# Output projection of a hybrid encoder layer: sixteen full blocks of w_out, or Strassen's seven half-size products

## The reference

```python
y_r = hr * jax.nn.silu(gr)                       # (tokens, 1024), RG-LRU group
y_c = (v @ cv_w2 + cv_b2) * jax.nn.silu(gc)      # (tokens, 1024), Conformer group
y = concat([y_r, y_c], -1) @ w_out               # w_out is (2048, 1024)
return x + rms_norm(y, post_g)                   # the norm runs over the 1024 outputs of a token
```

## Time and profile before

| | us |
|---|---|
| median of 3 executions | 828.98 |
| lowest and highest | 828.12, 829.11 |
| the profiled execution: its time | 828.99 |
| the profiled execution: its span | 827.0 |
| PE busy in that span | 804.9 |
| DVE, ACT, POOL busy | 571.2, 371.6, 259.0 |

### The profile page before, as it was taken

The page is one execution under the profiler, slowest core; times in us unless marked ns, Lnnn a source line. Parts: engine busy times, 40 slices in busy tenths (PEclk is TensorE's granted clock), DMA queues, the critical chain, the costliest instruction groups (busy, mean ns, idle before and its releaser), DMA issues. The chain is left out here.

```text
span 827.0 us, 12188 instructions
## 1 busy us (share of the span) xinstructions
PE 804.9 (97%) x4964; PEld 783.6 (95%) x4964; DVE 571.2 (69%) x510; ACT 371.6 (45%) x568; POOL 259.0 (31%) x156
## 2 busy tenths in 40 slices
PE   6999999999999999999999989899999999999996
PEld 4999999999999999999999978899999999999996
DVE  6589999999989959959959987962519322212225
ACT  6622482482482482482482458932517212211221
POOL 5224445446456455555464613010110000000000
PEclk8999999999999999999999999999999999999999
DMA  8311212202202302302302300423191111011047
GB/s 276 80 52 52 70 33 78 78 26 77 85 17 77 99 4 77 102 0 77 103 0 77 103 25 1 157 80 100 55 326 52 52 52 52 29 47 51 25 143 276
DMA packets 78737, 65.44 MB, mean 79 GB/s; under 512 B 2587, under 2 KB 71835, under 8 KB 78706
## 3 DMA queue, kind: packets, MB, share of 16 engines
q1 hardware_dynamic: 77776, 63.91, 23.9%
q0 software_dynamic: 928, 1.12, 0.6%
q10 hardware_dynamic: 2, 0.00, 0.0%
HBM read 51.77 MB, written 13.25 MB: 79 GB/s over the span
## 5 line engine op out<-in xcount | busy, mean ns | idle before, releaser
L731 PE MATMUL ps<-act_hi,w_hi 128*128 128x352 f32 (+5 forms) x1320 | 433.8, 329 | 1.1 <-DVE act_lo L1558 0.6
L733 PE MATMUL ps<-act_hi,w_lo 128*128 128x352 f32 (+5 forms) x1320 | 427.8, 324 | 0.0
L732 PE MATMUL ps<-act_lo,w_hi 128*128 128x352 f32 (+2 forms) x1128 | 366.0, 324 | 0.0
L1618 DVE SCALAR_TENSOR_TENSOR ps<-cv_in,par_cv,ps 128x1086 f32<-128x1086 f32 x232 | 313.8, 1353 | 7.8
L731 PEld LDWEIGHTS ps<-act_hi,w_hi 128*128 128x128 f32 x1320 | 248.5, 188 | 7.9 <-issue 6.8
L733 PEld LDWEIGHTS ps<-act_hi,w_lo 128*128 128x128 f32 x1320 | 248.6, 188 | 0.1
L732 PEld LDWEIGHTS ps<-act_lo,w_hi 128*128 128x128 f32 x1128 | 212.6, 188 | 0.4 <-issue 0.3
L586 POOL TENSOR_TENSOR w_lo<-wstage,w_hi 128x1024 fp32r<-128x1024 f32 x40 | 98.5, 2478 | 84.4 <-ACT w_hi L1064 84.2
L1064 ACT ACTIVATE w_hi<-wstage 128x1024 fp32r<-128x1024 f32 x63 | 65.7, 1054 | 101.4 <-PE ps L733 89.6
L1538 DVE TENSOR_TENSOR w_lo<-wstage,w_hi 128x1024 fp32r<-128x1024 f32 x24 | 30.3, 1262 | 60.5 <-ACT w_hi L1064 60.5
L731 PE MATMUL ps<-act_lo,w_hi 128*128 128x416 f32 (+2 forms) x192 | 63.4, 330 | 0.0
(11 more groups left out here) (193 smaller groups left out, 803.9 us busy)
## 6 DMA issues: line engine op xcount, KB each, us to landing
wstage<-in_w_in SPq DMA_DIRECT2D x40, 512.0 KB, 3.8
wstage<-in_w_out SPq DMA_DIRECT2D x16, 512.0 KB, 3.7
silu_spill<-silu_gc SPq DMA_DIRECT2D x8, 528.0 KB, 2.7
yr_spill<-y_rg SPq DMA_DIRECT2D x8, 528.0 KB, 2.7
silu_l<-silu_spill SPq DMA_DIRECT2D x8, 528.0 KB, 3.9
yr<-yr_spill SPq DMA_DIRECT2D x1, 4224.0 KB, 13.1
wstage<-in_cv_w_pw SPq DMA_DIRECT2D x8, 512.0 KB, 4.6
x_in<-in_x_prompt SPq DMA_DIRECT2D x7, 512.0 KB, 6.2
```

The lines of the kernel that those rows point to most:

```text
L731: pe.matmul(out, wh, xh, start=start, stop=False)
L732: pe.matmul(out, wh, xl, start=False, stop=False)
L733: return pe.matmul(out, wl, xh, start=False, stop=stop)
L1618: STT(out=acc, in0=src, scalar=w, in1=acc, op0=ALU.mult, op1=ALU.add).then_inc(taps, 1)
```

## The change

The 2 x 2 blocks (halves of the inputs by halves of the outputs) and the two halves of the tokens (`TH` = 528) are combined by Strassen's scheme: seven products of 1024 x 512 weights with 528 tokens in place of eight. Each product is four steps (`HT` = 4, one per output block), 28 steps in all, each of 8 k x 3 matmuls x 2 chunks of 264 columns. Five products use a sum or difference of two blocks of w_out, formed on POOL in place in one of five stages (`weight_sum`, 20 operations of 128 x 1024). Five use a sum or difference of operand halves, also on POOL (`operand_sum`, 40 operations of 128 x 528). The operand of every product is split anew on ACT and DVE, two k in each step (`next_operand_high`, `next_operand_low`), into `act_hi` and `act_lo` in turn. The first product uses y_r. The results are combined in `c_out` in SBUF: ACT copies, DVE adds or subtracts from PSUM (`add_product`). From step 12 on each step completes half a row: ACT squares it into the PSUM banks of the step, scales it in place, PE turns it (five transposes, `turn_half`), ACT copies the turned half back over the same row. Steps 26 and 27 run as four pieces of 272 and 256 columns.

```diff
-YCH = [(640, 416), (256, 384), (0, 256)]
+PRODUCTS = [((0, 0), ALU.add, (0, 1)), ((0, 1), ALU.subtract, (1, 1)), ((1, 1), None, None),
+            ((0, 0), ALU.add, (1, 1)), ((1, 0), ALU.add, (1, 1)), ((0, 0), None, None),
+            ((1, 0), ALU.subtract, (0, 0))]
+FINAL = 3 * HT
+PAIRED = STEPS - 2
...
+    def b_of(p, k):
+        if p == 1:
+            return c_half(HT + k // 2, k % 2)
+        return [y_r(k, 1), None, y_r(k, 0), y_r(k, 0), y_cv(k, 0), y_r(k, 1), y_cv(k, 1)][p]
...
@@ sync
+            def load_out(i):
+                s, second, (m, h) = BLOCKS[i]
+                if i < N_STAGE:
+                    if i < 2:
+                        sp.wait_ge(late_los, LATE_PW + 7 + i)
+                    elif i < 4:
+                        sp.wait_ge(pw, 6)
+                    else:
+                        sp.wait_ge(st_out, 16 * 6)
+                else:
+                    u, was_second, _ = BLOCKS[i - N_STAGE]
+                    if was_second:
+                        sp.wait_ge(wo_added, weight_sums(u))
+                    else:
+                        sp.wait_ge(late_los, LATE_OUT + u + 1)
...
@@ gpsimd
+            def weight_sum(s):
+                i, op = FIRST_BLOCK[s], PRODUCTS[s // HT][1]
+                if op is not None:
+                    for b in (i, i + 1):
+                        pool.wait_ge(wo_loaded[b % N_STAGE], 16 * (b // N_STAGE + 1))
+                    TT(OUT_STAGE[i % N_STAGE], OUT_STAGE[i % N_STAGE], OUT_STAGE[(i + 1) % N_STAGE], op)\
+                        .then_inc(wo_added, 1)
+            def operand_sum(p, k):
+                if p == 1:
+                    if k == 0:
+                        pool.wait_ge(yr_in, 16)
+                        pool.wait_ge(pw, KT)
+                        pool.wait_ge(yc, KT)
+                    TT(b_of(1, k), y_r(k, 0), y_r(k, 1), ALU.add).then_inc(b_sum, 1)
...
+            weight_sum(0)
+            weight_sum(1)
             pool.wait_ge(st_rows, 2)
...
+            for s in range(STEPS):
+                if s >= 2:
+                    weight_sum(s)
+                for k in (2 * (s % HT), 2 * (s % HT) + 1):
+                    operand_sum(s // HT + 1, k)
...
@@ tensor
+            def bank_free(s):
+                u = s - 2
...
+                elif u // HT in (0, 2):
+                    pe.wait_ge(c_copied, copies(u))
+                elif u // HT == 1:
+                    pe.wait_ge(c_added, additions(u))
+                else:
+                    pe.wait_ge(o_ssq, u - FINAL + 1)
+            for s in range(PAIRED):
+                p, ei = divmod(s, HT)
+                pe.wait_ge(late_los, LATE_OUT + s + 1)
+                bank_free(s)
+                for k in range(KT):
+                    if ei == 0:
+                        pe.wait_ge(b_low, p * KT + k + 1)
+                    for j in range(2):
+                        mm = step_product(s, k, j * TC, TC, 2 * (s % 2) + j)
...
+                    if k == 5 and s > FINAL:
+                        turn_half(s - 1)
@@ scalar
+            out_high(0)
             for k in range(KT):
+                operand_high(0, k)
+            out_high(1)
...
+            for s in range(PAIRED):
+                p, ei = divmod(s, HT)
+                out_high(s + 2)
+                act.wait_ge(oproj, s + 1)
...
+                next_operand_high(s)
@@ vector
+            out_low(0)
+            for k in range(KT):
+                operand_low(0, k)
             pw_out(KT - 1)
+            out_low(1)
+            next_operand_low(-1)
+            for s in range(PAIRED):
+                got = ps[:, 2 * (s % 2):2 * (s % 2) + 2, 0:TC]
+                dve.wait_ge(oproj, s + 1)
+                add_product(s, got)
+                out_low(s + 2)
+                if s >= FINAL:
+                    add_squares(s, got)
+                next_operand_low(s)
...
+                if s > 5 * HT:
+                    y_out(0, s - 5 * HT - 1)
...
+            STT(out=o_last, in0=ps[:, 3, 0:CHUNK_B[1]], scalar=par[:, KT - 1, P_PG:P_PG + 1], in1=c_scaled,
+                op0=ALU.mult, op1=ALU.add).then_inc(last_set, 1)
+            add_chunk(KT - 1, *CHUNK_B, 3, 4)
+            y_out(1, 1)
+            y_out(1, 2)
```

More of the change, by code:

```diff
@@ new lines, in b_hi, with b_lo @@
+    def b_hi(p, k):
+        return (act_hi, act_lo)[p % 2][:, k, 0:TH]
+    def b_lo(p, k):
+        return (act_hi, act_lo)[p % 2][:, k, TH:2 * TH]
+    ssq = [y_r(0, 0), y_r(1, 0)]
+    o_small = [yr[0:16, 2:4, 0:512], yr[0:16, 4:6, 0:512]]
+    X_HOME = [yr[:, 2 * i:2 * i + 2, TH:TH + 512] for i in range(4)] + [yr[0:16, 6:8, 0:512]]
+    for _r in (8, 9, 12, 10, 11):
+        X_HOME.append(act_x[:, _r, 0:D].rearrange("p (a n) -> p a n", a=2))
+    X_HOME[7] = act_x[0:16, 12, 0:D].rearrange("p (a n) -> p a n", a=2)
@@ L551, in _ @@
[L551 to L554, removed]
+            def load_out(i):
[13 more added lines that the diff above has]
+                        sp.wait_ge(late_los, LATE_OUT + u + 1)
+                e = m * HT + s % HT
+                sp.dma_start(OUT_STAGE[i % N_STAGE], w_out_v[:, (1 - h) * KT:(2 - h) * KT, e * P:(e + 1) * P])\
+                    .then_inc(wo_loaded[i % N_STAGE], 16)
@@ L555, in _ @@
+            for i in range(len(BLOCKS)):
+                if BLOCKS[i][0] == 5 * HT + 1 and BLOCKS[i][1] == 0:
+                    sp.wait_ge(b_low, 6 * KT)
+                    load_residual(0)
+                load_out(i)
+            sp.wait_ge(oproj, 6 * HT)
+            load_residual(1)
+            load_residual(2)
+            stores = 0
+            for j, tiles in enumerate(OUT_TILES):
+                for i, (c0, rows) in enumerate(tiles):
+                    n = TILE_BASE[j] + i
                     if j < 2:
@@ L957, in _ @@
                 mm.then_inc(pw, 1)
[L960 to L976, removed]
-                mm.then_inc(o_turned, 1)
@@ L979, in earlier_sums @@
[L979 to L1011, removed]
@@ new lines, in turn_tiles, with sums @@
+            def turn_tiles(j, src, bank):
+                for i, (c0, rows) in enumerate(OUT_TILES[j]):
+                    mm = pe.transpose(ps[0:rows, bank, i * P:(i + 1) * P], src[:, i * P:i * P + rows], ident[:, :])
+                mm.then_inc(o_turned, 1)
+            def sums(j, src, fst, last):
+                for i, (c0, rows) in enumerate(OUT_TILES[j]):
+                    mm = pe.matmul(ps[0:rows, 7, i:i + 1], src[:, i * P:i * P + rows], mean_w[:, 0:1],
+                                   start=fst and i == 0, stop=last, skip_group_check=True)
+                if last:
+                    mm.then_inc(ss_done, 1)
@@ new lines, in last_chunk, with turn_6a @@
+            def last_chunk(s, c0, n, bank, between):
+                for k in range(KT):
+                    mm = step_product(s, k, c0, n, bank)
+                    if k in between:
+                        between[k]()
+                mm.then_inc(oproj, 1)
+            half = STEPS - FINAL - 2
+            c_a = [c_half(e, 1)[:, CHUNK_A[0]:TH] for e in (KT - 2, KT - 1)]
+            c_b = c_half(KT - 2, 1)[:, 0:CHUNK_B[1]]
+            def turn_6a():
+                pe.wait_ge(o_scaled, half + 1)
+                pe.wait_ge(o_placed, half)
+                turn_tiles(1, c_a[0], 4)
@@ new lines, in sums_6a, with sums_turn_7a, turn_6b @@
+            def sums_6a():
+                pe.wait_ge(o_ssq, half + 1)
+                pe.wait_ge(ss_root, 5)
+                sums(1, ssq[1][:, CHUNK_A[0]:TH], True, False)
+            def sums_turn_7a():
+                pe.wait_ge(last_sqd, 1)
+                sums(1, last_sq[1], False, True)
+                pe.wait_ge(o_scaled, half + 2)
+                turn_tiles(1, c_a[1], 6)
+            def turn_6b():
+                pe.wait_ge(o_scaled, half + 3)
+                pe.wait_ge(o_placed, half + 1)
+                turn_tiles(2, c_b, 4)
@@ new lines, in sums_6b @@
+            def sums_6b():
+                pe.wait_ge(o_ssq, half + 2)
+                pe.wait_ge(ss_root, 5 + 3)
+                sums(2, ssq[1][:, 0:CHUNK_B[1]], True, False)
+            pe.wait_ge(late_los, LATE_OUT + PAIRED + 1)
+            pe.wait_ge(o_ssq, PAIRED - 2 - FINAL + 1)
+            last_chunk(PAIRED, *CHUNK_A, 0, {5: lambda: turn_half(PAIRED - 1)})
+            pe.wait_ge(late_los, LATE_OUT + PAIRED + 2)
+            pe.wait_ge(o_ssq, PAIRED - 1 - FINAL + 1)
+            last_chunk(PAIRED + 1, *CHUNK_A, 2, {5: turn_6a})
@@ L1512, in roots, with place_a @@
+            def place_a(e, bank):
+                A(c_half(e, 1)[:, 2 * P:4 * P], ps[:, bank, 0:2 * P], ACT.Copy)
+                A(o_small[1][:, e // 4, e % 4 * P:(e % 4 + 1) * P], ps[0:16, bank, 2 * P:3 * P], ACT.Copy)\
+                    .then_inc(o_placed, 1)
             def roots(j):
                 act.wait_ge(ss_done, j + 1)
-                n, whole = tile_base[j], sum(rows == P for c0, rows in out_tiles[j])
+                n, whole = TILE_BASE[j], sum(rows == P for c0, rows in OUT_TILES[j])
```

(63 more changed lines are left out.)

457 lines of the change are left out of this document (247 added, 210 removed).

## The result

The changed kernel took 839.38 us (median; 838.71 to 840.58) against 829.05 of the kernel before: a ratio of 1.0128 (95% interval 1.0112 to 1.0144), 1.3% slower. The forecast was 823.5 with a range of 814 to 835. The span of the profiled execution is 837.0 us, 10.0 more than before.

A forecast was written before the change was run, and what follows sets the result against it. PE's stream of matmuls was taken to set the end of the projection. Terms -22.7 + 3.5 + 1.6 + 4.0 + 3.7 + 1.6 + 1.0 + 1.8 = -5.5 us on 827.0 gave 823.5, range 814 to 835.

The forecast's parts named there:

- Middle: Later steps, including 16 to 19, 21 and 22: ACT, DVE and load delays mostly hidden, +1.0 us, bounds 0 and 6.
- PE's own work: PE's matmuls, transposes and small sums in the projection: 174.7 us after the change, -22.7 us.
- The start: Steps 0 to 7: later first weights, waits ahead of steps 1 and 2, slower steps 3 to 7, one clock loss.
- The wait of 1.6 ahead of step 1: Ahead of step 1: DVE's low weight part, behind other splits and against an operand sum, comes late, +1.6 us.
- The wait ahead of step 2: Ahead of step 2: late state transfers delay loads and POOL's operand sums delay its weight sum, +4.0 us.
- The turns: Steps 3 to 7: POOL and DVE alternate operation by operation, 6.6 us a step in place of 5.83, +3.7 us.
- The clock: Wait ahead of step 0 or 2: PE's granted clock falls to half pace once, +1.6 us.
- The tail: After the last matmul: DVE's scaled columns, add, y_out, copy and reciprocals delay the final outputs, +1.8 us.
- DVE as the bound: Rival: DVE's queue, waiting for whole POOL operations, sets 7.7 us in steps 3 to 7 and 16 to 19; 835, chance 0.22.
- The hidden turns: Rival: POOL runs at its faster pace, 5.8 us a step, no loss in steps 3 to 7; 815, chance 0.18.
- Short waits: Clock rival: waits ahead of steps 1 to 7 each bring a 1.6 us slow stretch; three more make 828.3, chance 0.07.
- Matmuls of 264 columns: Forecast 121 ns each; rival: they cost 138 ns and eat the gain, about 846, chance 0.03.

The follow-up runs named there:

- Experiment 1: Changed kernel with SP issuing the residual loads of the first output tiles 5 weight blocks later, ahead of step 25's block: 826.69 us, ratio 0.9972.
- experiment 3: Changed kernel with the edits of experiment 1 and experiment 2 together: 821.84 us, ratio 0.9917.
- experiment 2: Changed kernel with the first two w_out blocks loaded ahead of the yr reload and state transfers issued ahead of POOL's second weight sum: 833.19 us.
- experiment 5: On top of experiment 3, POOL forms the weight sum of step 2 ahead of the first four operand sums: 820.10 us, ratio 0.9889.
- experiment 6: On top of experiment 3, operand sums of products 2, 3, 5 and 6 over 16 of 528 columns, leaving out computation: 818.69 us.
- experiment 7: On top of experiment 3, DVE's low operand parts for products 1 and 2 over 16 of 528 columns, leaving out computation: 818.83 us.
- Experiment 4: Changed kernel with 40 idle transposes on PE ahead of step 0 and 24 ahead of step 2: 839.41 us, ratio 1.0118.

## Why the prediction was wrong

**The step that failed** stands under Middle: "Loads have a round of 3.7 + 2.4 + 1.1 + 1.2 = 8.4 us in two steps, 11.7: hidden", and with it the +1.0 with bounds 0 and 6. I priced the round of a load but not the queue that issues it. On SP the residual of the first tiles, with its own wait for the split of product 5, stands ahead of the weights of step 21, and I never listed that move. Measured: step 20 takes 17.9 us in place of 6.4. From step 8 to the last pieces it is 812.65 - 685.50 = 127.2 us, where 5 steps of 5.88 and 13 of 6.42 make 112.9. That is 14.3 over; 1.1 of it are the small sums of step 21, which belong to PE's own work, so 13.2 stand in place of the forecast's 1.0 (0.7 of them in step 18). Experiment 1 moved that wait and won 12.9 us. The prediction had named a wait of PE for scaled rows in steps 12 to 25 as a sign that it was wrong, and that is the wait that came, but from a cause that it had not thought of.

**PE's own work** was right: -22.7 forecast. By the measured paces 13 x 5.88 + 13 x 6.42 + 1.1 + 15.5 (the last pieces, 812.65 to 828.12) = 176.5 against 197.4: -20.9. Of the 1.8 us between them about 1.2 lie in the 26 steps, which took 159.9 in place of 158.7 with their transposes.

**The start** was forecast at 3.5 + 1.6 + 4.0 + 3.7 + 1.6 = 14.4 us and took 685.50 - 622.32 - 8 x 5.88 = 16.1. The 16.1 are 6.3 ahead of step 0, 2.3 in step 0, 3.2 in step 1 with the wait behind it, 1.6 in step 2 and 2.7 in steps 3 to 7. The size held, but not each cause, and that the errors nearly cancel is luck. PE came to step 0 some 0.8 us later than in the kernel before, and the wait ahead of it was 5.5 in place of 3.5: POOL's second weight sum did go ahead of DVE, the case for which the prediction had 627 and which it did not take, and DVE's subtraction beside it took 3.16 us in place of 1.23.

```profile
624.69 3.16 DVE L2009 TENSOR_TENSOR w_lo<-wstage,w_hi 128x1024 fp32r<-128x1024 f32 x1 [7.20 <-ACT w_hi L1613]
```

```profile
624.42 2.35 POOL L832 TENSOR_TENSOR w_stage<-w_stage 128x1024 f32<-128x1024 f32 x1 [0.90 <-DMA w_stage<-in_w_out]
...
634.21 6.93 POOL L842 TENSOR_TENSOR c_out<-yr 128x528 f32<-128x528 f32 x4 [4.41 <-DVE conv_out L1982]
641.11 2.37 POOL L832 TENSOR_TENSOR stage<-stage,wstage 128x1024 f32<-128x1024 f32 x1
```

The wait of 1.6 ahead of step 1 did not come, since step 0 ran slowly; in experiment 3, where step 0 has the full clock, it is there with 1.50. The wait ahead of step 2 was 3.1 in place of 4.0, and not for the states to land: POOL went from its four operand sums straight into `weight_sum(2)` at 641.11. Experiments 2, 3 and 5 say the same: issuing the states earlier left the wait, and moving the sum moved step 2 by 1.74 us but step 8 only by 0.42. From POOL's first operand sum on, the turns of POOL and DVE set step 8.

**The turns** were right: 6.6 us a step forecast, 6.63 to 6.66 measured in steps 4 to 6; experiments 5, 6 and 7 show them. As a term they cost 2.7 us in steps 3 to 7 (32.1 - 5 x 5.88) where 3.7 were forecast, since steps 3 and 7 took only 6.19 and 5.96. The rule of the Trainium skill (SBUF — State Buffer, SBUF: two separate sides), by which whichever of the two starts first blocks the other for the whole instruction, gives 7.7 by the prediction's prices; the rows of steps 5 and 6 say 6.6, and there the measurement decides. That the two hold each other up, as the page says, experiments 6 and 7 confirm.

**The clock** was mis-sized by its number, not its mechanism: one slow stretch of 1.6 us forecast, three seen, one behind each long wait. Step 2 took 1.6 us longer than 5.88, the size forecast, and step 0 took 2.3 longer. The Trainium skill's warning (TensorE: Matmul & The Clock Gate, HAM oscillation — how this bites in real kernels), that every long gap throttles anew, fits the trace (0.51, 0.57 and 0.53 in the three windows). Experiment 4 showed that the first of them was free, since step 2 waited anyway.

**The tail** was right: +1.8 forecast, 3.63 - 1.99 = 1.6 measured.

**The sum** of what was measured is -20.9 + 16.1 + 13.2 + 1.6 = +10.0 us, the growth of the span; the forecast was -22.7 + 14.4 + 1.0 + 1.8 = -5.5. Of the 15.5 us between them 12.2 are the middle.

**The rivals.** The slower rival, DVE as the bound, came near in time (835) and is still wrong: it asked for 7.7 us in steps 3 to 7, which took 6.7 at most, and with DVE's work unchanged experiment 1 takes all but 1.1 us from steps 20 and 21. In 16 to 19, where it asked for 5 us, only step 18 lost 0.7. The hidden turns asked for 5.8 in steps 3 to 7, and steps 4 to 6 took 6.6. Short waits did come ahead of steps 5 to 7, of 0.52 or 0.53 us, but no slow stretch with them: the granted clock is 1.00 from 651 to 680 us. Matmuls of 264 columns cost what the rows of 256 promised. Without the wait on SP the kernel takes 826.7 (experiment 1), 3.2 us above the forecast: with that step put right the rest of the sum would have held within its range.

## What to carry to other kernels

When an edit inserts a transfer with a wait of its own into a queue, write down what stands behind it in that queue and by when it is needed; a single misplaced group of residual loads cost 12.9 us here, more than half of what the seven products save on PE. Work moved to an idle POOL is not free if DVE reads two SBUF operands at the same time: add up the turns of both, not each engine's own time. And where such a sum set the pace here, reordering the queue gained little (0.42 us at step 8), while shorter operations on either side brought PE's pace back.

## What the runs showed of the hardware

- POOL and DVE operations that both read two SBUF tensors take turns. A POOL sum of 528 elements took 1.8 to 1.95 us on the mean among DVE's splits (experiment 3), where POOL's price alone was estimated at 1.33; one that met no such DVE operation for most of its time took 1.34 (changed kernel, at 636.32).
- 40 idle transposes in a wait of 5.5 us kept the granted clock at 2.4 GHz (1.00 in 625 to 635 us; without them 0.51 in 627 to 634), and changed the time by nothing that can be measured (839.41 against 839.38). 24 of them with a wait of 1.97 us behind them did not keep it (0.57 in 647 to 651 us).
